# First two passes of a fine-grained mixture of experts: three lanes, one of them given to an expert by a register address

## The reference

```python
scores = jax.nn.sigmoid(x.astype(jnp.float32) @ router.astype(jnp.float32))
sel = scores + router_bias.astype(jnp.float32)
grp = sel.reshape(sel.shape[:-1] + (N_GROUPS, N_EXPERTS // N_GROUPS))
gscore = jnp.sum(lax.top_k(grp, 2)[0], axis=-1)
_, gidx = lax.top_k(gscore, TOPK_GROUPS)                 # 4 of 8 groups
...
_, eidx = lax.top_k(jnp.where(emask, sel, -jnp.inf), TOP_K)   # 8 of 64 experts
...
h = jax.nn.silu(jnp.einsum('btd,edf->btef', x, w_gate)) * jnp.einsum('btd,edf->btef', x, w_up)
routed = jnp.einsum('btef,efd->btd', h * combine[..., None].astype(x.dtype), w_down)
shared = (jax.nn.silu(x @ ws_gate) * (x @ ws_up)) @ ws_down
```

## Time and profile before

| | us |
|---|---|
| median of 3 runs | 1386.15 |
| lowest, highest | 1386.1, 1397.01 |
| the profiled execution | 1386.34 |
| its span | 1384.4 |
| TensorE matmul busy | 1293.0 (93%) |
| VectorE busy | 465.1 (34%) |
| ScalarE busy | 342.9 (25%) |
| moved by DMA | 507.89 MB, mean 367 GB/s |

### The profile page before, as it was taken

How to read it: one execution, slowest core, us unless ns; L and a number is a source line. 1 busy time by engine, 2 the same in 40 slices (tenths; PEclk the granted TensorE clock), 3 DMA queues, 4 the chain that set the end, 5 groups by cost and what they waited for, 6 DMA issues and landing times.

```text
span 1384.4 us, 24011 instructions
## 1 busy us (share of the span) xinstructions
PE 1293.0 (93%) x9537; PEld 664.9 (48%) x9587; DVE 465.1 (34%) x1180; ACT 342.9 (25%) x695; POOL 18.5 (1%) x23
## 2 busy tenths in 40 slices
PE   6989999999999988989989999999999998898995
PEld 4757647444444444443444554644544444343442
DVE  2456624323222222222231363542222222222223
ACT  2167033211221211111231243422122112111212
POOL 2100000000000000000000000000000000000000
PEclk9999999999999999999999999999999999999998
DMA  9786899899999999999998465999999999999992
GB/s 355 216 330 246 329 369 368 336 406 403 420 421 420 420 421 420 421 421 421 415 388 301 161 220 187 365 366 398 411 420 420 421 419 421 420 421 420 421 420 119
DMA packets 112812, 507.89 MB, mean 367 GB/s; under 512 B 19004, under 2 KB 23296, under 8 KB 62656
## 3 DMA queue, kind: packets, MB, share of 16 engines
q1 hardware_dynamic: 111152, 502.37, 90.7%
q0 software_dynamic: 1008, 2.45, 0.5%
q10 hardware_dynamic: 544, 1.54, 0.3%
HBM read 504.18 MB, written 2.14 MB: 366 GB/s over the span
## 4 chain that ended last, share of the span: by engine, by line
PE 64%; DMA 24%; DVE 4%; SPq 4%; ACT 2%; issue 2%; ACTq 0%; DVEq 0%
PE PS L830 63%; DMA ring<-in_moe_w_up 12%; DMA W<-in_moe_w_up 8%; SPq L553 2%; DMA W<-in_mod_w 2%; DMA ring<-in_moe_w_down 2%; DMA ring<-in_mod_w 1%; DVE W L2078 1%; SPq L556 1%; DVE hT L1946 0%; PE PS L1081 0%; SPq L567 0%; PE PS L838 0%; PE PS L1407 0%; ACT W L1680 0%
## 5 line engine op out<-in xcount | busy, mean ns | idle before, releaser
L830 PE MATMUL PS<-ring,W 128*32 128x512 f32 (+5 forms) x3112 | 583.0, 577 | 27.3 <-DMA ring<-in_moe_w_up 13.2
L830 PE MATMUL PS<-W 128*128 128x128 bf16 (+7 forms) x3114 | 481.2, 366 | 13.1 <-DMA ring<-in_moe_w_up 7.2
L830 PEld LDWEIGHTS PS<-ring,W 128*32 128x32 f32 (+2 forms) x3112 | 180.7, 121 | 246.8 <-issue 232.3
L830 PEld LDWEIGHTS PS<-W 128*128 128x128 bf16 (+4 forms) x3114 | 224.0, 111 | 134.9 <-issue 124.7
L830 PE MATMUL PS<-W,junk 128*128 128x128 bf16 x848 | 116.6, 219 | 0.0
L2209 DVE TENSOR_TENSOR diag<-PS,diag 128x512 f32<-128x512 f32 x100 | 69.2, 692 | 139.9 <-ACT diag L1734 139.9
L830 PE MATMUL PS<-ring,hT 128*128 128x512 f32 x256 | 114.4, 596 | 0.7 <-issue 0.4
L2186 DVE SCALAR_TENSOR_TENSOR W<-W,PS 128x256 f32<-128x256 f32 x52 | 25.0, 480 | 262.3 <-ACT W L1721 262.3
L2203 DVE COPY W<-PS 128x512 f32<-128x512 f32 x53 | 36.7, 692 | 221.3 <-PE PS L830 221.3
L830 PE MATMUL PS<-diag,W 128*128 128x512 bf16 (+2 forms) x374 | 101.2, 394 | 8.9 <-issue 7.9
L1734 ACT CAST diag<-PS 128x512 bf16<-128x512 f32 x100 | 58.6, 586 | 191.2 <-PE PS L830 191.2
(11 more groups left out here) (275 smaller groups left out, 837.0 us busy)
## 6 DMA issues: line engine op xcount, KB each, us to landing
ring<-in_moe_w_down SPq DMA_DIRECT2D x104, 1024.0 KB, 24.2
ring<-in_moe_w_gate SPq DMA_DIRECT2D x88, 1024.0 KB, 20.7
ring<-in_moe_w_up SPq DMA_DIRECT2D x88, 1024.0 KB, 24.3
W<-in_moe_w_gate SPq DMA_DIRECT2D x41, 1024.0 KB, 21.0
W<-in_moe_w_up SPq DMA_DIRECT2D x41, 1024.0 KB, 24.6
W<-in_moe_w_down SPq DMA_DIRECT2D x25, 1024.0 KB, 24.4
ring<-in_mod_w SPq DMA_DIRECT2D x32, 768.0 KB, 8.7
ring<-in_mod_w SPq DMA_DIRECT2D x14, 1024.0 KB, 11.3
```

What stands on the lines that cost most here:

```text
L830: return eng.matmul(out, lhsT, rhs, start=first, stop=last, skip_group_check=True)
```

## The change

For passes 0 and 1 the two lanes of 64 slots become three: slots 0 to 31, slots 32 to 63, and slots 64 to 127. In pass `p` the second belongs to expert `2p` and the third to expert `2p + 1`. The first belongs to one of the two: to `2p` if it has more than 32 tokens (then both experts have 64 slots, as before), else to `2p + 1` (then that one has 96 slots and `2p` has 32). A flag per pass, made from the token counts, says which. It changes the places in lane 0, the weights of its slots (`chosen`), the number of columns that the plan counts for both experts (two more columns of `M`), and the weights that lane 0's matmuls read: TensorE loads the expert's number into a register (`open_lane`) and the moving operand's address in `ring` is worked out from it.

For this, TensorE gets two more matmul calls ahead of `ranks_done` and two register loads ahead of pass 0's products; `turn_slots` of pass 0 stands behind both `half_gate_up`, not ahead of them; VectorE gets more operations ahead of the one-hots; and `weight_parts`, with `pos_ready`, stands behind `nb_ready`. The diff, cut to its core (waits on `plan_dve` elsewhere only get their new numbers, since one step is added):

```diff
@@ constants
-C_N = C_STEP + 4
+C_SIGN = C_STEP + 4
+C_N = C_SIGN + RING // 2
+    for i in range(RING):
+        c[i, C_SIGN + i // 2] = 2.0 * (i % 2) - 1.0
-PLAN_DVE = {"keys_ready": 1, "cols_ready": 2, "nb_ready": 3, "m_cols_ready": 4}
+PLAN_DVE = {"keys_ready": 1, "lanes_ready": 2, "cols_ready": 3, "nb_ready": 4, "m_cols_ready": 5}
-        M, Mx, bM = c(COLS), c(XITEMS), c(XITEMS)
+        M, Mx, bM = c(COLS + RING // 2), c(XITEMS), c(XITEMS)
+        flags = c(2, RING // 2)
@@ gate_place, and down_place with 4096:6144
+            if not isinstance(q, int):
+                return ring[:, bass.ds(q, 1), 0:4096].rearrange("p a n -> p (a n)")
@@ lanes
-        def lanes(p, slots):
+        def lanes(p, slots, shared_lane=None):
+            if p < 2:
+                return [(0, 32, shared_lane), (32, 32, 2 * p), (64, 64, 2 * p + 1)]
@@ TensorE: pass_gate_up and pass_down
-                    gate_up(s, L * PASSES + p, lanes(p, GATE_SLOTS), wait_loaded)
+                    gate_up(s, L * PASSES + p, lanes(p, GATE_SLOTS, open_lane[p] if p < 2 else None), wait_loaded)
-                    down(s, L * PASSES + p, lanes(p, DOWN_SLOTS), wait_loaded)
+                    down(s, L * PASSES + p, lanes(p, DOWN_SLOTS, open_lane[p] if p < 2 else None), wait_loaded)
@@ TensorE: start of the stage
                 mm(PS[:, 4, E:2 * E], tri, mask[:, 1, :], False, True)
+                mm(PS[:, 4, 2 * E:2 * E + RING], ones, mask[:, 0, 0:RING], True, False)
+                mm(PS[:, 4, 2 * E:2 * E + RING], ones, mask[:, 1, 0:RING], False, True)
...
-                eng.wait_ge(s.pos_ready, L + 1)
-                turn_slots(s, 0, L * PASSES, 0)
+                eng.wait_ge(s.plan_dve, PLAN_DVE["lanes_ready"] + PLAN_STEPS * L)
+                open_lane = [eng.value_load(xtab[0:1, X_LANES + p:X_LANES + p + 1], min_val=0, max_val=RING - 1)
+                             for p in range(2)]
...
-                half_gate_up(L * PASSES, 0, lanes(0, GATE_SLOTS), s.plan_pe, list_experts)
-                half_gate_up(L * PASSES, 1, lanes(0, GATE_SLOTS), s.gu_done)
+                half_gate_up(L * PASSES, 0, lanes(0, GATE_SLOTS, open_lane[0]), s.plan_pe, list_experts)
+                half_gate_up(L * PASSES, 1, lanes(0, GATE_SLOTS, open_lane[0]), s.gu_done)
+                eng.wait_ge(s.pos_ready, L + 1)
+                turn_slots(s, 0, L * PASSES, 0)
                 shared_in(sh_gate_w[L], 0, 1, 4, KD).then_inc(s.sh_summed, 1)
@@ VectorE: start of the stage
                 dve.settle()
-                dve.keep(eng.tensor_scalar(places(0, 2 * STATIC, 0), pp[:, :, 0:STATIC], -1.0, None, ALU.add))
-                dve.keep(eng.tensor_scalar(places(0, 2 * STATIC, 1), pp[:, :, 0:STATIC], -33.0, None, ALU.add))
+                held = PS[:, 4, 2 * E:2 * E + RING].rearrange("p (e two) -> p e two", two=2)
+                ranks = [pp[:, :, i:RING:2] for i in range(2)]
+                lane = [posL[:, i:2 * RING:4, :].rearrange("p e s -> p s e") for i in range(4)]
+                shift = [rep[:, :, 2 * i:2 * i + 2] for i in range(2)]
+                dve.keep(eng.tensor_tensor(shift[0], ranks[1], ranks[0], ALU.subtract))
+                dve.keep(eng.tensor_scalar(flags[:, 0, :], held[:, :, 0], 32.5, None, ALU.is_lt))
+                for i in range(1, 4):
+                    dve.keep(eng.tensor_scalar(lane[i], ranks[i > 1], (-1.0, -33.0, -1.0)[i - 1], None, ALU.add))
+                dve.settle()
+                dve.keep(eng.scalar_tensor_tensor(out=shift[1], in0=shift[0], scalar=-32.0,
+                                                  in1=bc(flags[:, 0, :], 1, NS), op0=ALU.add, op1=ALU.mult))
+                dve.settle()
+                dve.keep(eng.scalar_tensor_tensor(out=lane[0], in0=ranks[0], scalar=-33.0, in1=shift[1],
+                                                  op0=ALU.add, op1=ALU.add))
                 dve.settle()
                 one_hots(s, 0, L * PASSES, 0)
...
-                weight_parts(paired(0, 2 * STATIC), bc(comb[:, :, 0:STATIC], 3, 2),
-                             com_rest[:, :, 0:2 * STATIC].rearrange("p s (e two) -> p s e two", two=2))\
-                    .then_inc(s.pos_ready, 1)
+                eng.tensor_tensor(xtab[0:1, X_LANES:X_LANES + 2], iota[0:1, 0:RING:2], flags[0:1, 0, :], ALU.add)\
+                   .then_inc(s.plan_dve, 1)
+                for sub in range(2):
+                    dve.keep(eng.tensor_scalar(places(2 * RING, 2 * STATIC, sub), pp[:, :, RING:STATIC], -1.0 - 32 * sub,
+                                               None, ALU.add))
+                dve.keep(eng.tensor_tensor(M[0:E, COLS:], con[0:E, C_SIGN:C_SIGN + RING // 2], flags[0:E, 0, :], ALU.mult))
+                dve.keep(eng.tensor_scalar(flags[:, 1, :], flags[:, 0, :], -1.0, 1.0, ALU.mult, ALU.add))
                 copy_gathered(s, L * PASSES)
...
                 eng.tensor_reduce(nb[0:E, 0, 4:5], nb[0:E, 0, 0:4], AX, ALU.add).then_inc(s.plan_dve, 1)
+                held = [comb[:, :, i:RING:2] for i in range(2)]
+                chosen = rep[:, :, 16:16 + 2 * STATIC]
+                for i in range(2):
+                    dve.keep(eng.tensor_tensor(shift[i], held[i], bc(flags[:, 1 - i, :], 1, NS), ALU.mult))
+                for i in range(1, 4):
+                    dve.keep(eng.tensor_copy(chosen[:, :, i:2 * RING:4], held[i > 1]))
+                dve.keep(eng.tensor_copy(chosen[:, :, 2 * RING:].rearrange("p s (e two) -> p s e two", two=2),
+                                         bc(comb[:, :, RING:STATIC], 3, 2)))
+                dve.settle()
+                dve.keep(eng.tensor_tensor(chosen[:, :, 0:2 * RING:4], shift[0], shift[1], ALU.add))
+                dve.settle()
+                weight_parts(lambda q: com3[:, :, 0:2 * STATIC, q], chosen, com_rest[:, :, 0:2 * STATIC])\
+                    .then_inc(s.pos_ready, 1)
                 copy_slots(s, L * PASSES, wT[0])
                 eng.wait_ge(s.plan_pe, PLAN_PE["ids_done"] + 6 * L)
                 eng.tensor_copy(xtab[0:1, 0:COLS], PS[0:1, 3, 128:128 + COLS]).then_inc(s.xtable_ready, 1)
```

More of the change, by code:

```diff
@@ L175 @@
 """.split()
-PLAN_DVE = {"keys_ready": 1, "cols_ready": 2, "nb_ready": 3, "m_cols_ready": 4}
+PLAN_DVE = {"keys_ready": 1, "lanes_ready": 2, "cols_ready": 3, "nb_ready": 4, "m_cols_ready": 5}
+PLAN_STEPS = len(PLAN_DVE)
 PLAN_PE = {"keys_spread": 1, "ids_done": 2, "gate_done": 3, "hi_done": 4, "table_done": 5, "extra_done": 6}
@@ L324, in trunk @@
         xtab = xtab_place.bitcast(I32)
-        X_IDS, X_COUNT = COLS, COLS + XITEMS
+        X_IDS, X_COUNT, X_LANES = COLS, COLS + XITEMS, COLS + XITEMS + 1
         c = Carve()
@@ L473, in gate_place @@
         def gate_place(q):
+            if not isinstance(q, int):
+                return ring[:, bass.ds(q, 1), 0:4096].rearrange("p a n -> p (a n)")
             return ring[:, q, 0:4096] if q < RING else place4[:, 0:4096] if q == RING else place5
         def down_place(q):
+            if not isinstance(q, int):
+                return ring[:, bass.ds(q, 1), 4096:6144].rearrange("p a n -> p (a n)")
             return ring[:, q, 4096:6144] if q < RING else place4[:, 4096:6144]
@@ L1212, in moe @@
                 gather(s, L * PASSES, S[0])
-                eng.wait_ge(s.plan_dve, PLAN_DVE["keys_ready"] + 4 * L)
+                eng.wait_ge(s.plan_dve, PLAN_DVE["keys_ready"] + PLAN_STEPS * L)
                 mm(PS[0:E, 3, 64:128], ones[0:E, 0:E], key[0:E, :], True, True).then_inc(s.plan_pe, 1)
-                eng.wait_ge(s.pos_ready, L + 1)
-                turn_slots(s, 0, L * PASSES, 0)
+                eng.wait_ge(s.plan_dve, PLAN_DVE["lanes_ready"] + PLAN_STEPS * L)
+                open_lane = [eng.value_load(xtab[0:1, X_LANES + p:X_LANES + p + 1], min_val=0, max_val=RING - 1)
+                             for p in range(2)]
                 def list_experts():
-                    eng.wait_ge(s.plan_dve, PLAN_DVE["cols_ready"] + 4 * L)
-                    mm(PS[0:1, 3, 128:128 + COLS], ecol[0:E, :], M[0:E, :], True, True).then_inc(s.plan_pe, 1)
+                    eng.wait_ge(s.plan_dve, PLAN_DVE["cols_ready"] + PLAN_STEPS * L)
+                    mm(PS[0:1, 3, 128:128 + COLS], ecol[0:E, :], M[0:E, 0:COLS], True, True).then_inc(s.plan_pe, 1)
                 eng.wait_ge(s.xg_act, L * PASSES + 1)
@@ L1235, in plan_spread @@
                     ins.then_inc(s.ppT_turned, 1)
-                    eng.wait_ge(s.plan_dve, PLAN_DVE["nb_ready"] + 4 * L)
+                    eng.wait_ge(s.plan_dve, PLAN_DVE["nb_ready"] + PLAN_STEPS * L)
                     eng.wait_ge(s.xtable_ready, 2 * L + 1)
@@ L1245, in plan_table @@
                         at = st * 2 * COLS
-                        mm(PS[:, 2, at:at + COLS], ppT[0:E, st * P:(st + 1) * P], M[0:E, :], True, True)
+                        mm(PS[:, 2, at:at + COLS], ppT[0:E, st * P:(st + 1) * P], M[0:E, 0:COLS], True, True)
                         ins = mm(PS[:, 2, at + COLS:at + 2 * COLS], combT[0:E, st * P:(st + 1) * P],
```

(8 more changed lines are left out.)

## The result

| | before | after |
|---|---|---|
| median, us (4 runs each) | 1386.12 | 1430.57 |
| lowest to highest | 1385.54 to 1397.01 | 1429.32 to 1431.52 |
| ratio to before, 95% interval | | 1.031 [1.0288, 1.0333] |
| the profiled execution, its span | 1386.34, 1384.4 | 1431.52, 1429.4 |

The forecast was 1377.5 with a range of 1372 to 1384 and a chance of 0.02 for slower by over 1%. It is wrong by 53 us.

What follows compares the result with a forecast made beforehand. Loads bound each layer's end, with TensorE setting the pace in early passes. 1386.3 - 15.05 (layer 1's tail) + 2 x 2.7 (layer starts) + 1.0 (load queue) = 1377.6, rounded to 1377.5; range 1372 to 1384.

Steps and rivals of the forecast that it cites:

- What bounds the kernel: Loads bound each layer's end, but TensorE paces them early, so its time in passes 0 and 1 counts in full.
- Step 4: Pass 0's gate and up products: three lanes, one register-addressed, run side by side; +0.8 us per layer, 0 to 2.2.
- The rule that was weighed: TensorE issue: about 62 ns per matmul if decoded in software; some 8 us over both layers, time about 1384 if exposed.
- Step 4's register term: Pass 0's gate and up: one register operation per step, 0.14 us each over 16 steps; 0.8 taken, 0 to 2.2.
- The rival of slow register matmuls: 64 register-addressed matmuls each stop TensorE's queue: 1385 us at 0.14 each, 1395 at 0.3; chance 0.10.
- Steps 1 and 2: Layer start: two more TensorE products, +0.5 us; more VectorE work before the one-hots, +0.27 and +0.4; gather about 0.8 later.
- Step 3: Before pass 0's gate products: two register loads on TensorE, `turn_slots` moved away; +1.0 us per layer, 0.55 to 1.5.
- Step 5: After pass 0's up products: `turn_slots`, slot weights and ids come there, delaying `turn_hidden`; +0.9 us per layer.
- Steps 1 to 5: All new work at each layer's start: +2.7 us per layer, from 1.45 to 4.6.
- The wait on the load queue: Refills on SP wait for late ids: 8.2 us later, 5.5 behind schedule; layer 0 catches up, layer 1 keeps 0 to 3.1.
- The 1.0 kept for layer 1: The part of the load queue's delay that layer 1 does not make good: 1.0 us taken, from 0 to 3.1.
- The tail: End of layer 1: expert 1's extra item vanishes, so the write of `x` starts 15.05 us sooner.

Runs made afterwards that it cites:

- the flag kernel: Changed kernel with four lanes of 32 and the flag always 0, so the extra item runs again: 1390.05 us, ratio 1.0021 to the kernel before.

## Why the prediction was wrong, point by point

- **What bounds the kernel: right, and it is why the loss counts in full.** TensorE's time in passes 0 and 1 goes to the end of the layer: 28.5 us more in the products became 27.9 and 29.4 us more in the mixture. TensorE waited for no load in the 80 us from pass 1, as the prediction had said.
- **Step 4 failed.** It said that lanes of 32 beside lanes of 64 run side by side in later passes. No row carried that, and the code said otherwise: kind A is two lanes of 64, B and D are four of 32; no pass of the kernel before has both. From there "a third lane costs nothing in the array" was an assumption, and it got no bound. The measured price of the step is 10.9 us in gate and up of pass 0 alone, against 0 to 2.2. The prediction went on to say that pass 1 and the downs cover what is new; there the mixed lanes cost another 17.6 us.
- **The rule that was weighed was not the one that bore on the change.** The prediction weighed a rule on the issue of matmuls. The runs agree with it in their times: 1.14 us per step against 0.45, 0.13 us per change, and no overlap between the two widths. What the array does at a change no trace shows. As a rival, the case of widths that take turns could have been priced from the rows of before: 16 steps of 256 columns take 7.5 us; pass 1's gate and up have as many columns, each down half as many, so with every step paid twice a layer grows by 7.5 + 7.5 + 3.75 + 3.75 = 22.5 us before any price of a change, and the time is 1377.5 + 45 = 1422.5. That would have turned the sign.
- **Step 4's register term (0.8 taken, 0 to 2.2) measured about 0.1.** Four lanes of 32 take 7.52 us for the 16 steps with the register address, and 7.52 in the kernel before with constants. The one difference is at the start: the first product begins 0.90 us after the copy out of the gather with the register address and 0.79 with constants (919.98 to 920.88, 920.22 to 921.01; the same in layer 0). The rival of slow register matmuls is out.
- **Steps 1 and 2 right in size, too little cover seen.** From the last operation on `comb` ahead of the ranks to `pp` 1.82 against 1.43 us: +0.39 (0.5 said). From `pp` to the one-hots 1.21 against 0.61: +0.60 (0.67 said). But the gather followed 0.57 after the one-hots and not 1.11, so it came 0.45 later and not 0.8.
- **Step 3 over-sized.** The gate products start 0.90 us after the copy out of the gather starts, before 1.10: with `turn_slots` gone they are sooner, and no time of the two register loads is seen. No run leaves out the loads alone. All in all they start 0.25 later, not 1.0.
- **Step 5: 0.64, not 0.9.** `turn_hidden` comes 2.40 us after the up products (900.91 to 903.31), before 1.76. Steps 1 to 5 together: 0.9 us per layer and not 2.7. The totals allow a little more: the flag kernel's 2.9 us (1.7 to 4.3) for both layers stand against the prediction's 6.4, so it had about doubled this part.
- **The wait on the load queue: right.** Relative to the copy, SP's first refill comes 11.36 us after it and not 5.40 (four lanes of 32): 6.0 late, and with the later copy 6.4 in all, against 8.2 said; 0.9 of it is the shift of steps 1 to 5 (2.7 said), which leaves 5.5 as said. It is made good, in layer 1 too. The 1.0 kept for layer 1 does not show.
- **The tail: right** at 15.05, and so was the reading that one item of expert 1 in layer 1 is what goes.

With the one step mended in the kernel (four lanes of 32), 1375.55 was measured against the forecast of 1377.5. By ratios that is 0.9926 [0.9904, 0.9947] against 1377.5 / 1386.3 = 0.9937. The rest of the mechanism was right, and its costs were taken some 3 us too high.

A sentence of the prediction on what would show it did fire: it named steps above 0.6 us, "or slow ones in pass 1 too", as a sign for slow register matmuls. The steps were there and the cause was another; the weight loads by width told them apart.

## What to carry to other kernels

When an edit brings lanes of another width into a pass, look for a pass in the trace that mixes exactly these widths before costing it at nothing; if there is none, the bound is that each width runs alone, and each change of width costs something besides (0.13 us here). Cut all lanes of a pass to the narrowest width: two lanes of 32 cost what one of 64 costs, and the mixture stays parallel. A claim like "as in later passes" needs its row like any number.

## What the runs showed of the hardware

- fp32 matmuls on column tiles of 32 and of 64, all on 128 rows, do not overlap: a step of 256 columns takes 1.14 us and not 0.45, one of 512 columns 1.99 and not 0.88. Tiles of one width do: 16 steps of 256 columns take 7.5 us with two lanes of 64, three of 32 or four of 32, and 8 steps of 512 columns take 7.0 us with one lane of 64 alone and 7.1 with two of 64 or four of 32.
- Each change between the widths costs about 0.13 us on top, whether matmuls of 256 or of 512 columns lie between.
- A moving operand whose address comes from a register costs TensorE nothing per step (7.52 us for 16 steps with and without), and about 0.1 us once ahead of the first product of a layer. The two register loads are not seen either: 0.2 us lie between the end of the copy (893.18) and the first product (893.39).
